# First two query units of the memory attention: multiplying the sum before its norm, with the norm settled on their outputs

## The chip, the cores and the metric

The kernel runs on one core of one Trainium2 chip. The metric is the device time of one execution, in microseconds (us). Below, TensorE is PE, its weight load PEld, VectorE DVE, ScalarE ACT, GpSimd POOL and SyncE SP.

## What is computed

Two transformer layers follow one another on a sequence of 256 tokens of width 1024. Only this part of the first layer matters here:

```python
h = hybrid_mixer(x, ...)                        # ends in  concat @ w_out
x = layer_norm(ALPHA * x + h, ln1_g, ln1_b)     # the first norm
h = memory_cross_attention(x, mem, wq, wkv, wo) # q = x @ wq, softmax(q k^T / 16) v @ wo
x = layer_norm(ALPHA * x + h, ln2_g, ln2_b)
```

with `layer_norm(x) = (x - mean) * rsqrt(var + eps) * g + b`, the mean and variance of a token taken over its 1024 values. The result is needed in f32 quality.

## The kernel before

**Tiling.** Activations lie transposed: 128 rows of the width by 256 tokens, eight such blocks (`k` = 0 to 7) for the 1024 values. `X` holds the stream in f32. Each input of a product is split into a high and a low half in the matmul's own format (`INH`, `INL`, or `HIH`, `HIL`), and each weight chunk likewise (`hir`, `lor`), so that one product is three matmuls: high by high, high by low, low by high (`three`, L521).

**Weights.** A weight chunk is 512 KB: four blocks of 128 rows by 256 columns, loaded by SP to one of six buffers `raw`, rounded by ACT to `hir` (L1103), and the rest taken by DVE to `lor` (L1608, `split`). There are four `hir`/`lor` slots. A unit, such as `("xq", 0)`, is two chunks and makes 256 output columns in one PSUM bank: 48 matmuls. The class `Ahead` sets, on ACT and on DVE alike, at which place of the program a split stands: before the work on a unit's output, up to three chunks further on (`AHEAD = 3`), as far as a slot is free in the order of the program. Between them lie 48 chunks of `mod_wT`, which DVE multiplies and sums (L1625). The order on each engine is so fixed by the text; an engine that waits for one instruction holds all behind it.

**The stretch.** Four `wout` units end the mixer. After each one DVE adds its output to `X` (`resid`, L1611), ACT squares the sum (L1250), and DVE keeps running sums over the blocks (`stats`). In `layer_norm("n1")` PE then sums the columns (`row_sums`), DVE works out mean and factor on 2 columns (L1878 to L1886), PE spreads each to a bank of 256 tokens (`spread_bank`), DVE subtracts the one and multiplies by the other (L1608, `X<-X,ps`), ACT applies gain and bias twice, once to `INH` (L1269) and once to `X` (L1274), and DVE takes the low half `INL`. Then come the query units: `xq 0` and `xq 1` interleaved block by block, so that PE has 12 matmuls for each block of `x1`, then `xq 2` and `xq 3`. DVE copies each output to `QC` (L1926). From there the four heads of the attention go through a chain from PE (logits `lx`) to DVE (maximum, L1939), ACT (exponential, L1294), DVE (L1943, scaling) and PE.

The third norm, before the second layer, already does what the change brings here, in a larger form: its units `("q", 2)` and `("k", 2)` multiply `X` by a gain (`xg`, `late_g`), and the norm is settled on the outputs (L2127 to L2131, L1405).

Of the kernel before, what the change touches and what calls it, by code (L numbers as in the profile page):

```python
# [14 lines left out]
T = 256  # L15
# [310 lines left out]
UNITS = ((0, 1), (1, 1), (2, 2), (4, 2), (6, 2))  # L326


def build(nc, A, out):
    with ExitStack() as ctx:  # L330
# [19 lines left out]
        HIH = sb("HIH", 22 * TE, F32R)[:, :].rearrange("p (k t) -> p k t", t=TE)[:, :, 0:T]  # L350
        HIL = sb("HIL", 22 * TE, F32R)[:, :].rearrange("p (k t) -> p k t", t=TE)[:, :, 0:T]
# [83 lines left out]
        SN = SMALL[:, 424:436]  # L435
        SS, VP, VR4, SD4, RR = (CH[:, a:a + n] for a, n in ((0, 4), (4, 2), (6, 2), (8, 2), (10, 2)))
# [12 lines left out]
        xg = Inp("xg", INHX, INLX)  # L449
        mem, hid, hd = (Inp(n, HIH, HIL) for n in ("mem", "hid", "hd"))  # L450
# [32 lines left out]
        def last_matmul(i):  # L483

            (key, k0), _, n, kind = plan[i]
            if k0 + n < ends[key]:
                return "read", i
            return ("unit", key, 1) if kind == "wide" or key in (("q", 2), ("k", 2)) else ("unit", key)
# [24 lines left out]
        def tensor(e):  # L513
# [24 lines left out]
            def units_g(keys, kt, x, outs=columns):  # L538
                bs = [lin.get(("unit", key), bank) for key in keys]
# [29 lines left out]
            def unit(key, kt, x, outs=columns):  # L569
                run(units_g([key], kt, x, outs))  # L570
# [30 lines left out]
            def late_g(keys, x, n):  # L601
                bs = [[p.get(("unit", key, j), bank, hold=True) for j, p in enumerate((lin, att))] for key in keys]
                w.wait_ge(act.at(("xg", "hi ext")), dve.at(("xg", "lo ext")))
# [201 lines left out]

            for c in range(4):
                unit(("wout", c), 8, mix)
            mm.mark("x1 free")
            layer_norm("n1")

            mm.mark("before cross attention")
            run(units_g([("xq", 0), ("xq", 1)], 8, x1))
            unit(("xq", 2), 8, x1)
            unit(("xq", 3), 8, x1)
            mm.mark("oc free")

            for i in range(6):
                if i < 4:
                    b, before = att.get(("lx", i), bank)
                    w.wait_ge(copied(before), dve.at(("QC", i)), act.at("KV"))  # L820
# [262 lines left out]
        def scalar(e):  # L1083
# [192 lines left out]

            for c in range(4):
                ahead.unit(("wout", c), 8)
                square("n1", c, X[:, 2 * c:2 * c + 2, :], dve.at(("n1", "x", c)), squares_free("n1", None, c))
                if c == 2:  # L1280
                    preload(ACT.Sqrt)
            layer_norm("n1", "ln1_g", "ln1_b", x1, "x1 free")

            act.mark("before cross attention")
            ahead.units([("xq", 0), ("xq", 1)], 8)
# [317 lines left out]
        def vector(e):  # L1603
# [310 lines left out]

            for c in range(4):
# [3 lines left out]
            layer_norm("n1", "ln1_g", "ln1_b", x1, "x1 free")  # L1919

            dve.mark("before cross attention")
            before = [mm.at("before cross attention"), dve.at("before cross attention"), act.at("before cross attention")]

# [680 lines left out]
```

## Time and profile before

| | us |
|---|---|
| median of three runs | 903.06 |
| lowest and highest of them | 900.4, 904.37 |
| the profiled execution | 901.49 |
| its span, first to last instruction | 899.7 |

| engine | busy, share of the span |
|---|---|
| PE | 95% |
| PEld | 90% |
| DVE | 72% |
| ACT | 56% |

Shares are averages over stages with different limits. In the chain of work that ended last, PE has 63% of the span, DVE 14% and ACT 7%. What the change is worth is read in its own stretch, some 40 us from the last `wout` unit to the first maximum of the attention.

### The profile page before, as it was taken

What the parts mean: (1) busy time and instruction counts of PE and PEld (TensorE: products, weight loads), DVE (VectorE), ACT (ScalarE), POOL (GpSimd) and SP (SyncE); (2) the same over time, 40 slices, a digit from 0 to 9 for tenths busy, and PEclk for the clock granted to TensorE, in tenths of its full rate; (3) what the DMA queues carried; (4) which work ended last, traced back from release to release, by engine and by line L of the source; (5) the groups of instructions that cost most, each with busy time, mean ns of one, the idle gap of its engine ahead of it and who ended that gap; (6) DMA issues with size and microseconds to landing.
All of it is one profiled execution on the core that took longest, in us unless ns stands there. A gap on an engine that the chain in (4) does not pass through costs nothing.

```text
span 899.7 us, 15840 instructions
## 1 busy us (share of the span) xinstructions
PE 857.0 (95%) x6396; PEld 807.8 (90%) x6396; DVE 651.3 (72%) x1011; ACT 503.2 (56%) x723; POOL 7.6 (1%) x17
## 2 busy tenths in 40 slices
PE   8989998999899999999997989999899899999997
PEld 7869987889799999999996989898899899999886
DVE  5765697678668888887867896687797866665453
ACT  5644447355447666655446657777657654444442
POOL 0200000000000000000000000000000000000000
PEclk9989999989998999999988999999999799999999
DMA  9973567747062766567752576475575276775751
GB/s 337 241 226 104 160 229 221 212 154 238 24 184 74 231 186 185 174 208 255 260 188 70 154 222 200 129 224 166 160 225 175 66 250 219 233 233 186 162 212 47
DMA packets 139592, 166.89 MB, mean 186 GB/s; under 512 B 5520, under 2 KB 123280, under 8 KB 139520
## 3 DMA queue, kind: packets, MB, share of 16 engines
q1 hardware_dynamic: 137712, 162.82, 57.8%
q0 software_dynamic: 720, 2.02, 1.2%
q8 instruction: 50, 0.82, 0.4%
q10 hardware_dynamic: 1088, 1.05, 0.3%
q14 instruction: 22, 0.18, 0.1%
HBM read 164.62 MB, written 1.25 MB: 184 GB/s over the span
## 4 chain that ended last, share of the span: by engine, by line
PE 63%; DVE 14%; ACT 7%; issue 3%; DVEq 0%; ACTq 0%
PE ps L519 62%; DVE lor L1608 5%; DVE FA L1608 3%; ACT hir L1103 2%; DVE FA L1611 1%; DVE FA L1614 1%; DVE X L1608 1%; DVE INL L1608 1%; DVE raw L1625 0%; ACT FA L1294 0%; ACT L1447 0%; ACT FA L1227 0%; ACT FA L1489 0%; DVE X L1611 0%; ACT L1118 0%
## 5 line engine op out<-in xcount | busy, mean ns | idle before, releaser
L1608 DVE TENSOR_TENSOR lor<-raw,hir 128x1024 fp32r<-128x1024 f32 (+1 forms) x267 | 309.8, 1177 | 115.2 <-ACT hir L1103 110.2
L1103 ACT ACTIVATE hir<-raw 128x1024 fp32r<-128x1024 f32 (+1 forms) x257 | 260.3, 1032 | 124.9 <-PE ps L519 104.4
L519 PE MATMUL ps<-INH,hir 128*128 128x256 f32 (+1 forms) x1064 | 306.7, 288 | 4.2 <-ACT INH L1269 2.5
L519 PE MATMUL ps<-INH,lor 128*128 128x256 f32 (+1 forms) x1064 | 302.5, 284 | 3.4 <-DVE lor L1608 3.4
L519 PE MATMUL ps<-INL,hir 128*128 128x256 f32 (+1 forms) x1064 | 303.2, 285 | 1.2 <-DVE INL L1608 0.9
L519 PEld LDWEIGHTS ps<-INH,hir 128*128 128x128 f32 x1064 | 204.7, 192 | 7.4 <-issue 5.8
L519 PEld LDWEIGHTS ps<-INH,lor 128*128 128x128 f32 x1064 | 204.4, 192 | 5.4 <-DVE lor L1608 4.4
L519 PEld LDWEIGHTS ps<-INL,hir 128*128 128x128 f32 x1064 | 204.0, 192 | 2.5 <-DVE INL L1608 2.4
L519 PE MATMUL ps<-HIH,lor 128*128 128x256 f32 x688 | 195.9, 285 | 4.3 <-DVE lor L1608 4.3
L519 PE MATMUL ps<-HIH,hir 128*128 128x256 f32 x688 | 198.2, 288 | 0.0
L519 PE MATMUL ps<-HIL,hir 128*128 128x256 f32 x688 | 194.6, 283 | 0.0
L519 PEld LDWEIGHTS ps<-HIH,lor 128*128 128x128 f32 x688 | 131.0, 190 | 6.1 <-DVE lor L1608 5.3
L519 PEld LDWEIGHTS ps<-HIH,hir 128*128 128x128 f32 x688 | 131.3, 191 | 3.9 <-issue 3.0
L519 PEld LDWEIGHTS ps<-HIL,hir 128*128 128x128 f32 x688 | 131.6, 191 | 0.0
L1611 DVE SCALAR_TENSOR_TENSOR FA<-ps,vec,FA 128x254 f32<-128x254 f32 (+2 forms) x130 | 53.2, 473 | 15.2 <-ACT FA L1113 15.2
L519 PE MATMUL ps<-hir,HIH 128*128 128x512 f32 (+1 forms) x136 | 52.8, 388 | 6.5 <-DVE HIL L1608 6.5
L1625 DVE SCALAR_TENSOR_TENSOR raw<-raw,cb 128x1024 f32<-128x1024 f32 x48 | 58.2, 1218 | 0.6 <-DMA raw<-in_mod_wT 0.6
L519 PE MATMUL ps<-lor,HIH 128*128 128x512 f32 (+1 forms) x136 | 52.3, 384 | 0.0
L519 PE MATMUL ps<-hir,HIL 128*128 128x512 f32 (+1 forms) x136 | 52.2, 384 | 0.0
L1113 ACT ACTIVATE FA<-ps,vec 128x256 f32<-128x256 f32 x58 | 29.3, 556 | 30.4 <-PE ps L519 30.4
L519 PE MATMUL ps<-FA 128*128 128x256 f32 (+6 forms) x212 | 39.2, 365 | 4.2 <-DVE FA L1608 3.4
L1608 DVE TENSOR_TENSOR HIL<-FA,HIH 128x512 fp32r<-128x512 f32 (+2 forms) x34 | 23.4, 689 | 23.8 <-ACT HIH L1108 23.2
(270 smaller groups left out, 792.8 us busy)
## 6 DMA issues: line engine op xcount, KB each, us to landing
raw<-in_w_in SPq DMA_DIRECT2D x64, 512.0 KB, 4.7
raw<-in_mod_wT SPq DMA_DIRECT2D x48, 512.0 KB, 4.5
raw<-in_ffn_w_up SPq DMA_DIRECT2D x44, 512.0 KB, 4.6
raw<-in_w_ffn_in SPq DMA_DIRECT2D x44, 512.0 KB, 4.7
raw<-in_w_ffn_out SPq DMA_DIRECT2D x22, 512.0 KB, 4.6
raw<-in_ffn_w_down SPq DMA_DIRECT2D x20, 512.0 KB, 4.8
raw<-in_xa_wkv SPq DMA_DIRECT2D x16, 512.0 KB, 4.2
raw<-in_xa_wq SPq DMA_DIRECT2D x8, 512.0 KB, 4.9
```

The costliest lines, as they stand in the source:

```text
L519: return e.matmul(o, l, r, start=start, stop=stop, skip_group_check=True)
L1103: e.activation(hi, src, ACT.Copy).then_inc(*w_hi.up(i))
L1113: e.activation(o[:, b, :], p[:, b * T:(b + 1) * T], ACT.Identity, scale=V(wname, (K - 1) * nb + i + b), bias=V(bname, i + b)).then_inc(*ac ...
L1608: return e.tensor_tensor(o, a, b, op)
L1611: return e.scalar_tensor_tensor(out=o, in0=a, scalar=s, in1=b, op0=op0, op1=op1)
L1614: return e.tensor_scalar(o, a, s1, s2, op0, op1) if op1 else e.tensor_scalar(o, a, s1, None, op0)
L1625: e.scalar_tensor_tensor(out=v, in0=v, scalar=1.0, in1=CB[:, :], op0=MUL, op1=MUL, accum_out=MOD[:, key[1]:key[1] + 1]).then_inc(*dve.up(key))
```

## The change

The first two query units no longer read the normed `x1` but a new input `xg1` = `X` times `ln1_g`, before the norm. With G = diag(g), the query is ((x - mean) / dev * g + b) W = (x G W - mean * (g W)) / dev + b W. Two extra columns beside the 256 tokens hold g and b themselves, so that the same matmuls (258 columns) give gW and bW.

- **In the `wout` loop**, after each unit ACT makes two blocks of `xg1.hi` (128x256 each, `gained`) and DVE the two of `xg1.lo`. Before the loop ACT and DVE each write the two extra columns (`gains`). `xg1` lies in `HIH`/`HIL`, blocks 0 to 7.
- **PE** runs one step of the two units (12 matmuls: two units, two halves of 128 columns) before the column sums, one between sums and mean, one between mean and factor, and five behind it. Each unit uses two banks, one of `lin`, one of `att`.
- **The norm itself stays**, since `x1` is needed by `xq 2`, `xq 3` and the residual. It goes in four pairs of blocks instead of 1, 1, 2, 2, 2; the mean row is copied by ACT to `MB` first; gain and bias of all eight blocks are applied to `X` by ACT, none by DVE.
- **The splits** of the following weight chunks stand at other places: one and a `mod` product before the first subtraction, two and a `mod` product between the second and the third pair, one behind the norm, one between the two settlings.
- **Settling**, per unit, replaces the copy to `QC` (128x512): DVE does a copy of two columns and a 128x256 multiply-subtract for each half, then a 128x512 multiply; ACT negates and adds bW, twice 128x256. The logits of heads 0 and 1 wait for ACT's part.

The core of the diff:

```diff
+        xg1, xg2 = (Inp(n, HIHX[:, 0:8, :], HILX[:, 0:8, :]) for n in ("xg1", "xg2"))
...
+            def late_norm(name, keys, x):
+
+                g = late_g(keys, x, 2)
+                steps_of(g, 1)
+                row_sums(name, 3, X[:, 6:8, :])
+                steps_of(g, 1)
+                spread_bank((name, "mu"), SN[:, 0:2])
+                steps_of(g, 1)
+                spread_bank((name, "r"), SN[:, 6:8])
+                run(g)
...
-            layer_norm("n1")
-
             mm.mark("before cross attention")
-            run(units_g([("xq", 0), ("xq", 1)], 8, x1))
+            late_norm("n1", LATE[0], xg1)
             unit(("xq", 2), 8, x1)
-            unit(("xq", 3), 8, x1)
+            unit(("xq", 3), 8, x1, pool=att)
+            late_free(LATE[0])
```

ACT, and below it DVE:

```diff
+            def gained(x, name, gn, c, free):
+                for k in (2 * c, 2 * c + 1):
+                    w.wait_ge(dve.at((name, "x", c)), vec_in.at(0), mm.at(free))
+                    e.activation(x.hi[:, k, 0:T], X[:, k, :], ACT.Copy, scale=V(gn, k)).then_inc(*act.up((x.name, "hi", k)))
...
+                for k in (0, 2, 4, 6):
+                    if k == 4:
+                        run(late)
...
+            def settle(i, key, dst):
+                for j in range(2):
+                    w.wait_ge(dve.at((key, "normed")))
+                    e.activation(dst[:, j, :], dst[:, j, :], ACT.Identity, scale=-1.0, bias=GB2[i][j][:, 1:2]).then_inc(*act.up((key, "settled")))
...
+            for c in range(2):
+                settle(c, ("xq", c), QC[:, 2 * c:2 * c + 2, :])
+                if c == 0:
+                    ahead.more()
```

```diff
+                for k in (0, 2, 4, 6):
+                    d = X[:, k:k + 2, :]
+                    w.wait_ge(act.at((name, "mean row")), act.at((x.name, "hi", k + 1)), dve.at((x.name, "lo", k + 1)))
+                    tt(d, d, over(MB, 2), SUB).then_inc(*dve.up())
+                    w.wait_ge(mm.at((name, "r")), dve.last())
+                    tt(d, d, over(br[:, 0:T], 2), MUL).then_inc(*dve.up((name, "normed", k), ("out", (name, "r"))))
+                    if k:
+                        low(k - 2)
+                    if k == 2:
+                        run(late)
+                low(6)
+                ahead.more()
...
-            query(0)
-            query(1)
```

The order on the engines follows from this. PE, from the end of the last `wout` unit; before:

```order
L519 MATMUL ps<-HIL,hir 128x256
L519 MATMUL ps<-con,st 128x1
L519 MATMUL ps<-con,SQ 128x1
L519 MATMUL ps<-con,st 128x1
L519 MATMUL ps<-con,SQ 128x1
L519 MATMUL ps<-con,X 128x1 x4
L519 MATMUL ps<-con,SQ 128x1 x4
L519 MATMUL ps<-con,small 128x128 x4
L519 MATMUL ps<-INH,hir 128x256
```

PE at the same place after the change:

```order
L523 MATMUL ps<-HIL,hir 128x258
L523 MATMUL ps<-con,st 128x1
L523 MATMUL ps<-con,SQ 128x1
L523 MATMUL ps<-con,st 128x1
L523 MATMUL ps<-con,SQ 128x1
L523 MATMUL ps<-con,X 128x1 x4
L523 MATMUL ps<-con,SQ 128x1 x4
L523 MATMUL ps<-HIH,hir 128x258
```

Twelve matmuls of 258 columns now stand ahead of the column sums, and twelve between them and the spreading of the mean; `con,small` is a spread.

ACT from the first normed block to the table load for the exponential; before:

```order
L1269 ACTIVATE INH<-X,vec 128x256 x4
L1274 ACTIVATE X<-X,vec 128x256 x2
L1269 ACTIVATE INH<-X,vec 128x256 x2
L1274 ACTIVATE X<-X,vec 128x256 x2
L1269 ACTIVATE INH<-X,vec 128x256 x2
L1274 ACTIVATE X<-X,vec 128x256 x2
L1103 ACTIVATE hir<-raw 128x1024 x7
L1294 ACT_TABLE_LOAD
```

ACT after the change, from the second pair of blocks on:

```order
L1322 ACTIVATE INH<-X,vec 128x256 x2
L1326 ACTIVATE X<-X,vec 128x256 x2
L1124 ACTIVATE hir<-raw 128x1024 x2
L1322 ACTIVATE INH<-X,vec 128x256 x2
L1326 ACTIVATE X<-X,vec 128x256 x2
L1322 ACTIVATE INH<-X,vec 128x256 x2
L1326 ACTIVATE X<-X,vec 128x256 x2
L1124 ACTIVATE hir<-raw 128x1024
L1333 ACTIVATE FA<-FA,small 128x256 x2
L1124 ACTIVATE hir<-raw 128x1024
L1333 ACTIVATE FA<-FA,small 128x256 x2
L1124 ACTIVATE hir<-raw 128x1024 x3
```

Two of the seven splits moved ahead of the third pair, and each settling (`FA<-FA,small`) stands between splits.

DVE behind the last low halves of `x1`; before:

```order
L1608 TENSOR_TENSOR INL<-X,INH 128x2x256 x2
L1625 SCALAR_TENSOR_TENSOR raw,small<-raw,cb 128x1024
L1608 TENSOR_TENSOR lor<-raw,hir 128x1024 x2
L1625 SCALAR_TENSOR_TENSOR raw,small<-raw,cb 128x1024
L1926 COPY FA<-ps 128x512 x2
L1608 TENSOR_TENSOR lor<-raw,hir 128x1024 x2
L1625 SCALAR_TENSOR_TENSOR raw,small<-raw,cb 128x1024
L1608 TENSOR_TENSOR lor<-raw,hir 128x1024
L1926 COPY FA<-ps 128x512
L1608 TENSOR_TENSOR lor<-raw,hir 128x1024 x2
L1926 COPY FA<-ps 128x512
L1939 TENSOR_REDUCE small<-ps 128x2
```

DVE after the change; behind these rows come the multiply that ends the second settling, a `mod` product, a split, the copy of `xq 2`, two splits, the copy of `xq 3` and the first maximum:

```order
L1670 TENSOR_TENSOR INL<-X,INH 128x2x256 x2
L1670 TENSOR_TENSOR lor<-raw,hir 128x1024
L2027 COPY small<-ps 128x2
L1673 SCALAR_TENSOR_TENSOR FA<-st,small,ps 128x256
L2027 COPY small<-ps 128x2
L1673 SCALAR_TENSOR_TENSOR FA<-st,small,ps 128x256
L1670 TENSOR_TENSOR FA<-FA,ps 128x512
L1670 TENSOR_TENSOR lor<-raw,hir 128x1024
L2027 COPY small<-ps 128x2
L1673 SCALAR_TENSOR_TENSOR FA<-st,small,ps 128x256
L2027 COPY small<-ps 128x2
L1673 SCALAR_TENSOR_TENSOR FA<-st,small,ps 128x256
```

The two copies of queries 0 and 1 became two settlings of five instructions each, and three splits that stood behind them now stand elsewhere: two before the third pair, one between the settlings.

## Rows read from the trace of the kernel before

**Rows 1.** The page: busy time, share of the span and instructions of each engine.

```profile
PE 857.0 (95%) x6396; PEld 807.8 (90%) x6396; DVE 651.3 (72%) x1011; ACT 503.2 (56%) x723; POOL 7.6 (1%) x17
```

**Rows 2.** Windows: start:end, length, then busy time of each engine, granted clock.

```profile
167.60:190.40 22.80, 22.80 (x194) 22.75 (x193) 17.85 (x24) 12.09 (x15) 0.00 (x0) 1.00 0.84 254
190.40:197.50 7.10, 5.15 (x34) 4.43 (x32) 3.76 (x12) 2.38 (x4) 0.00 (x0) 0.77 0.50 150
222.90:238.00 15.10, 12.42 (x63) 10.10 (x63) 8.66 (x24) 6.17 (x20) 0.00 (x0) 1.00 0.23 82
```

**Rows 3.** Timeline, PE: start us, busy us, what; column sums, spreads, first query matmul.

```profile
191.86 1.05 PE L519 MATMUL ps<-con,X 128*128 128x1 f32 x8 [0.51 <-DVE X L1611]
...
194.06 2.25 PE L519 MATMUL ps<-con,small 128*128 128x128 f32 x8 [0.26 <-DVE small L1878]
197.56 0.55 PE L519 MATMUL ps<-INH,hir 128*128 128x256 f32 x1 [1.24 <-ACT INH L1269]
```

**Rows 4.** Timeline, DVE, from the last residual to the first maximum.

```profile
188.85 2.36 DVE L1608 TENSOR_TENSOR lor<-raw,hir 128x1024 fp32r<-128x1024 f32 x2 [0.57 <-ACT hir L1103]
191.13 0.68 DVE L1611 SCALAR_TENSOR_TENSOR X<-X,ps 128x512 f32<-128x512 f32 x1
193.85 0.16 DVE L1878 COPY small<-ps 128x4 f32<-128x4 f32 x1 [2.04 <-PE ps L519]
194.87 0.17 DVE L1886 RECIPROCAL small<-small 128x2 f32<-128x2 f32 x1 [0.27 <-ACT small L1264]
...
203.77 1.40 DVE L1608 TENSOR_TENSOR X<-X,ps 128x512 f32<-128x512 f32 x2
...
207.53 0.69 DVE L1608 TENSOR_TENSOR INL<-X,INH 128x512 fp32r<-128x512 f32 x1 [1.76 <-ACT X L1274]
...
222.92 0.69 DVE L1926 COPY FA<-ps 128x512 f32<-128x512 f32 x1 [0.36 <-PE ps L519]
224.64 0.69 DVE L1939 TENSOR_REDUCE small<-ps 128x2 f32<-128x512 f32 x1 [1.04 <-PE ps L519]
```

**Rows 5.** Timeline, ACT: table load and splits of the loop's end, the norm, the splits.

```profile
186.30 1.28 ACT L1118 ACT_TABLE_LOAD   x1
187.70 1.99 ACT L1103 ACTIVATE hir<-raw 128x1024 fp32r<-128x1024 f32 x2
191.84 0.63 ACT L1250 ACTIVATE SQ<-X 128x512 f32<-128x512 f32 x1 [2.15 <-DVE X L1611]
...
201.83 1.08 ACT L1269 ACTIVATE INH<-X,vec 128x256 fp32r<-128x256 f32 x2
202.94 1.09 ACT L1274 ACTIVATE X<-X,vec 128x256 f32<-128x256 f32 x2
```

**Rows 6.** Timeline, PE at the third norm: sums, matmuls after them, spreads, a wait.

```profile
467.99 0.95 PE L519 MATMUL ps<-small,X 128*128 128x3 f32 x8
...
470.58 0.43 PE L519 MATMUL ps<-INH,hir 128*128 128x260 f32 x1
...
474.35 0.28 PE L519 MATMUL ps<-INH,hir 128*128 128x260 f32 x1
...
477.38 0.61 PE L519 MATMUL ps<-con,small 128*128 128x128 f32 x4
```

**Rows 7.** Timeline, DVE and ACT at the third norm: gained blocks, one settling.

```profile
455.36 0.87 DVE L1611 SCALAR_TENSOR_TENSOR INL<-X,small,INH 128x256 fp32r<-128x256 f32 x2
...
497.60 0.15 DVE L2127 COPY small<-ps 128x3 f32<-128x3 f32 x1
...
499.50 0.15 DVE L2127 COPY small<-ps 128x3 f32<-128x3 f32 x1
```

**Rows 8.** Timeline, ACT at the third norm: gained blocks, row copy, settling.

```profile
452.08 0.90 ACT L1362 ACTIVATE INH<-X,small 128x256 fp32r<-128x256 f32 x2
...
476.16 0.60 ACT L1374 ACTIVATE st<-ps 128x512 f32<-128x512 f32 x1 [1.99 <-PE ps L519]
...
502.51 1.71 ACT L1405 ACTIVATE FA<-FA,small 128x256 f32<-128x256 f32 x4 [6.56 <-DVE FA L1611]
```

More of the change, by code:

```diff
@@ L487, in last_matmul @@
                 return "read", i
-            return ("unit", key, 1) if kind == "wide" or key in (("q", 2), ("k", 2)) else ("unit", key)
+            return ("unit", key, 1) if kind == "wide" or any(key in keys for keys in LATE) else ("unit", key)
         before_in_slot, seen = {}, {}
@@ L536, in halves, with units_g @@
                 return act.at((x.name, "hi", k)), dve.at((x.name, "lo", k))
-            def units_g(keys, kt, x, outs=columns):
-                bs = [lin.get(("unit", key), bank) for key in keys]
+            def units_g(keys, kt, x, outs=columns, pool=lin):
+                bs = [pool.get(("unit", key), bank) for key in keys]
                 oo = [outs(b) for b, _ in bs]
@@ L567, in units_g, with unit @@
                         yield
-            def unit(key, kt, x, outs=columns):
-                run(units_g([key], kt, x, outs))
+            def unit(key, kt, x, outs=columns, pool=lin):
+                run(units_g([key], kt, x, outs, pool))
             def wide_g(key, kt, x, pool=lin, apart=0):
@@ new lines, in settle @@
+            def settle(name, i, key, dst, *free):
+                br = bank[name, "r"]
+                for j in range(2):
+                    b, vs = bank["unit", key, j], GB2[i][j]
+                    w.wait_ge(mm.at(("unit", key, j)))
+                    e.tensor_copy(vs, b[:, T:T + 2]).then_inc(*dve.up())
+                    w.wait_ge(dve.last(), act.at((name, "mean row")), *free)
+                    stt(dst[:, j, :], MB, vs[:, 0:1], b[:, 0:T], MUL, SUB).then_inc(
+                        *dve.up(("out", ("unit", key, j))))
+                w.wait_ge(dve.last(), mm.at((name, "r")))
+                tt(dst, dst, over(br[:, 0:T], 2), MUL).then_inc(*dve.up((key, "normed"), ("out", (name, "r"))))
@@ L1915, in vector @@
+            gains(xg1, "ln1_g", "ln1_b")
             for c in range(4):
@@ L1918, in vector @@
                 stats("n1", c, None)
-            layer_norm("n1", "ln1_g", "ln1_b", x1, "x1 free")
+                gained(xg1, "ln1_g", c)
             dve.mark("before cross attention")
             before = [mm.at("before cross attention"), dve.at("before cross attention"), act.at("before cross attention")]
+            late_norm("n1", xg1, x1, "x1 free", LATE[0])
+            for c in range(2):
+                settle("n1", c, ("xq", c), QC[:, 2 * c:2 * c + 2, :], *before)
+                if c == 0:
+                    ahead.more()
             def query(c):
```

71 lines of the change are left out of this document (64 added, 7 removed).

## The prediction

> **What bounds the kernel now.** I read the page first: PE is busy 95% of the span, DVE 72%, ACT 56% [rows 1]. The windows then say where this stretch differs. In the `wout` units PE is busy without a gap at full clock; in the 7.1 us of the norm it does little, and its mean granted clock is 0.77 [rows 2]. The PE timeline shows that hole from its side: column sums at 191.86, spreads at 194.06, the first query matmul at 197.56 after 1.24 us of waiting for ACT's first normed block [rows 3]. This is what the change fills. But the timelines of the other two engines have to be read on to the first maximum of the attention at 224.64 [rows 4]. Behind it, to 238, PE has 12.4 of 15.1 us busy by short pieces, and PE, DVE and ACT wait for each other in turn, with each head's maximum, exponential and scaling in one chain [rows 2]. That chain starts with DVE's maximum, which stands behind all of DVE's work of the stretch. So the time is set by when DVE reaches it, and whatever moves that start moves the end of the kernel by as much: nothing of the order behind it is changed. Before, DVE came to it early: it waited 0.36 us for the last query unit and 1.04 us for the logits [rows 4].
>
> **Durations used.** In a row of independent instructions each takes its busy time less some 0.09 us. A split is 1.14 us on DVE (two at 2.36) and 0.95 on ACT (two at 1.99) [rows 4, 5]. A 128x512 operation of DVE is 0.61, and 0.70 where the next depends on it (1.40 for two) [rows 4]. A gained block is 0.40 on ACT and 0.40 on DVE [rows 7, 8]. Gain and bias of a pair of blocks are four ACT instructions of 0.50, some 2.1 us [rows 5]. One settling on DVE is 1.9 us, from 497.60 to 499.50; ACT's half of it takes 0.85, half of the 1.71 for two units [rows 7, 8]. Here the settling is one instruction shorter in its second part, not in these 1.9.
>
> **Part 1, the `wout` loop.** ACT gets 8 gained blocks, DVE 8: 3.2 us on each, and 0.3 for the extra columns. In the first loops idle time hides most: DVE waits there for ACT and PE. What counts is the last loop. The 2 gained blocks of unit 2 stand ahead of ACT's table load (1.28 us) and that ahead of two splits; and the gained blocks of the two loops before have by then made the third residual 0.9 us late, since DVE's waits there don't hide all of them. ACT's splits start at 189.3 instead of 187.70 [rows 5]. DVE's two splits follow, 190.4 to 192.7, and the last residual starts at 192.7 instead of 191.13 [rows 4]: **+1.5**. PE meanwhile does its first 12 matmuls and the early column sums, so its wait costs nothing. Column sums end at 195.3, and DVE's copy comes at 195.35 against 193.85; its two last gained blocks lie in that wait.
>
> **Part 2, mean and factor.** PE now runs 12 matmuls ahead of each spread. After the column sums of the third norm the granted clock fell to the lower of its two levels, 1.2 of 2.4 GHz: from 470.58 to 474.35 17 matmuls took 3.8 us, 0.22 each; then 0.12 each [rows 6]. I take the same here, since sums and waits last from 192.4 to 195.3. The mean is spread after 12 slow matmuls, at 197.9, and ACT's copy of the row (bounded by 0.60 for twice the size, I take 0.46) ends at 199.2 [rows 8]. The factor comes after 12 more, partly slow, at 200.4, with its spread (0.61 [rows 6]) done at 201.0. DVE in the meantime has done one split and one `mod` product, to 198.7. It subtracts at 199.2 and multiplies at 201.0. Before, the third pair's subtraction and multiplication, the last ones, began at 203.77 and six blocks were done [rows 4]; now at 201.6 only two are. With the clock at full the factor would come 1.6 earlier.
>
> **Part 3, the rest of the norm.** ACT has 2.1 us for each pair, all eight blocks, and it is in series with DVE: pairs one and two take it from 201.7 to 206.0. Only then do the two splits of `xq 2` stand in its queue, 206.0 to 207.9. DVE, done with the first low half at 204.6, waits **2.5 us** for the first of them. Then two splits and the `mod` product run from 207.1 to 210.5, ahead of the last two pairs; the last low half starts at 216.3 against 207.53 before [rows 4]. Of that, 3.4 us are splits that stood behind the norm before; 5.4 are the late start and the waits.
>
> **Part 4, settling.** DVE: split of `xq 3` at 217.3 (ACT's half from 216.2), settling 0 from 218.4 to 220.3. ACT's part of it runs to 221.3; the next split is behind it in ACT's queue, and DVE waits for that until 222.4: **2.1 us**. Split to 223.5, settling 1 to 225.4, `mod` product to 226.6; ACT's part of settling 1 again stands ahead of its split, so DVE waits 0.9. Split 227.5 to 228.6, copy of `xq 2` 0.6, two splits 2.3: the copy of `xq 3` starts at 231.5 and the maximum at 232.1.
>
> **PE in the same stretch.** Its late units end at 208.1; `xq 2` begins at 208.4 and waits for low halves at 212.6, 214.9 and 217.1; `xq 3` waits for its second chunk until 223.6 and ends at 226.7, or 228.3 if the clock falls in the waits. With some 1.9 us of logits PE is done before DVE's maximum at 232.1: PE's own delay costs nothing. The SP queue is no bound: a chunk is loaded when the split six chunks ahead of it is done, and the first `xo` chunk, due at 227.5, is asked for at 208.3.
>
> **The sum.** 232.1 - 224.64 = **+7.5 us**. As a balance: +1.5 late residual; DVE work added behind it 0.8 (two gained blocks) + 3.8 (settlings) - 1.2 (two copies) - 1.1 (smaller pieces of the norm, two affine steps) = +2.3; waits of DVE 11.2 us against 7.5 before (5.5 of them in [rows 4]), +3.7. Against the profiled execution 901.49 + 7.5 = 909.0; against the median of 903.06 it is 910.5, and I take 910.0 between them. Bounds: with no clock loss after the sums 5.9, with twice as long a one 8.1. If row and split times err by 0.1 us in each of the dozen handovers, another 1.2 either way.
>
> **Rivals.**
> - **The hole fills and PE sets the time (faster).** PE's work from 190.41 is 192 matmuls of 0.12 (23.0), sums 2.9, spreads 1.1 and 1.6 for the slow clock: end at 219.0 instead of 222.9, **-3.9**, 898.5. It holds if DVE and ACT keep ahead of PE. For it: PE is the busiest engine and the hole is real [rows 1, 3]. Against it: DVE has 28.3 us of work from the late residual at 192.7 on (the 33.5 us of before less 7.5 of waits, plus 2.3), so even without any wait it reaches the maximum only at 221.0. Chance 0.08. The Trainium skill says the same as this rival (Perfetto Trace Analysis, Identifying the Most-Contended Engine and Optimization Strategy): optimize the engine with the highest occupancy first, and for TensorE by its weight-load share; find its gaps and make what it waits for start sooner. By that rule the change gains; the rows of DVE speak against it, since the engine that is late next is not the one with the gap.
> - **Waits of ACT and DVE overlap better (between).** If the two waits behind ACT's gain work and settling (2.5 and 2.1) are half as long and the clock holds, +3 to +5, 904.5 to 907.5 on the median's scale. It decides if ACT's queue is emptier than I count: its pairs at 2.1 us are measured [rows 5]. Chance 0.16.
> - **The change does nothing that can be seen.** The late units would have to hide exactly what they add. Chance 0.04.
> - **More is lost.** PE's waits of 2 to 3 us at `xq 2` and `xq 3` lower the clock; with late reads ACT's splits for `xo` come later, and low clock into the attention adds to its short matmuls: +10 to +12, 913 to 915. The clock stood at 1.00 there before [rows 2]. Chance 0.06.
>
> **How the numbers follow.** My forecast, +6 to +9, has the remaining 0.66. What a measurement of this kernel can tell from no change is about 0.5%, 4.5 us. Slower by more: 0.66 + 0.06 + a part (0.06) of the between case = 0.78. Within: 0.10 of that case, 0.04 and 0.01 of the first = 0.15. Faster: 0.07. The range of 8 in 10 leaves out the gain and the far end: 905 to 914.
>
> **What would show it.** In the changed profile: the last residual of the loop 1.5 us later relative to the end of `wout`; PE busy through most of the old hole, with matmuls of 258 columns at 0.42 us busy after the sums; DVE idle for `hir` 2 to 3 us ahead of the splits between the second and third pair, and again 2 us between the settlings; the last copy of a query unit on DVE with no wait for PE ahead of it, and the first maximum some 41.5 us after the last `wout` matmul instead of 34. Wrong, if PE's last query matmul is what the maximum waits for, or if ACT's splits stand ready when DVE comes to them.

## The result and the profile after

| | us |
|---|---|
| before, median of eight runs | 902.76 |
| after, median of eight runs | 911.06 |
| ratio, 95% interval | 1.009, 1.0067 to 1.0114 |
| profiled execution of after, and its span | 909.77, 908.0 |

The change makes the kernel slower by 0.9%, some 8.1 us. A second measurement, beside other runs of before, gave 911.21 and the ratio 1.0107 (1.0087 to 1.0127), 9.6 us.

The page of after, busy time and share of each engine, beside [rows 1]: every share is within 1 point of before, and the time is 8 us longer. The shares alone tell nothing here.

```profile
PE 859.7 (95%) x6396; PEld 810.5 (89%) x6396; DVE 655.7 (72%) x1024; ACT 509.1 (56%) x740; POOL 7.6 (1%) x17
```

More is told by the windows of the stretch, from DVE's last residual to its first maximum. The columns are those of [rows 2]. First before, then after:

```profile
191.13:224.64 33.51, 31.34 (x227) 29.78 (x228) 25.52 (x42) 17.81 (x25) 0.00 (x0) 0.90 0.58 188
```

```profile
191.90:232.91 41.01, 34.71 (x229) 32.68 (x227) 27.87 (x47) 21.23 (x34) 0.00 (x0) 0.88 0.45 143
```

DVE has 2.35 us more work in it and waits 13.1 us instead of 8.0. PE's busy time grew by 3.4 us for nearly the same number of matmuls (229 against 227), with a mean granted clock of 0.88 instead of 0.90.

The timeline of DVE in after, from the last residual to the first maximum (start, busy time, what; in brackets the wait ahead and who ended it). It answers [rows 4]:

```profile
191.90 0.68 DVE L1673 SCALAR_TENSOR_TENSOR X<-X,ps 128x512 f32<-128x512 f32 x1
195.56 0.16 DVE L1992 COPY small<-ps 128x4 f32<-128x4 f32 x1 [1.00 <-PE ps L523]
199.62 0.69 DVE L1670 TENSOR_TENSOR X<-X,st 128x512 f32<-128x512 f32 x1 [0.58 <-ACT st L1315]
201.61 0.69 DVE L1670 TENSOR_TENSOR X<-X,ps 128x512 f32<-128x512 f32 x1 [1.30 <-PE ps L523]
...
207.75 2.36 DVE L1670 TENSOR_TENSOR lor<-raw,hir 128x1024 fp32r<-128x1024 f32 x2 [2.47 <-PE ps L523]
...
216.98 0.69 DVE L1670 TENSOR_TENSOR INL<-X,INH 128x512 fp32r<-128x512 f32 x1 [1.42 <-ACT X L1326]
...
223.16 1.23 DVE L1670 TENSOR_TENSOR lor<-raw,hir 128x1024 fp32r<-128x1024 f32 x1 [2.02 <-ACT hir L1124]
...
228.30 1.23 DVE L1670 TENSOR_TENSOR lor<-raw,hir 128x1024 fp32r<-128x1024 f32 x1 [0.88 <-ACT hir L1124]
229.44 0.69 DVE L2050 COPY FA<-ps 128x512 f32<-128x512 f32 x1
230.05 2.35 DVE L1670 TENSOR_TENSOR lor<-raw,hir 128x1024 fp32r<-128x1024 f32 x2
232.31 0.69 DVE L2050 COPY FA<-ps 128x512 f32<-128x512 f32 x1
232.91 0.68 DVE L2060 TENSOR_REDUCE small<-ps 128x2 f32<-128x512 f32 x1
```

The last two copies of query units and the maximum have no wait ahead of them: PE had been done. The 2.47 us are put down to PE, though the splits' `hir` halves were ACT's work from 206.57 on, behind the gain and bias of the second pair (in the trace of run 4 the same wait of 2.47 us is put down to ACT). ACT in after, the places where it stands in DVE's way:

```profile
206.57 1.99 ACT L1124 ACTIVATE hir<-raw 128x1024 fp32r<-128x1024 f32 x2
...
221.18 0.91 ACT L1333 ACTIVATE FA<-FA,small 128x256 f32<-128x256 f32 x2 [3.28 <-DVE FA L1670]
221.99 1.04 ACT L1124 ACTIVATE hir<-raw 128x1024 fp32r<-128x1024 f32 x1
```

PE in after, beside [rows 3]: a wait for the last split, sums of columns, the second late step, spreads, and at last the attention's first transposes (L853) and the matmuls behind them.

```profile
190.95 0.36 PE L523 MATMUL ps<-HIH,hir 128*128 128x258 f32 x1 [0.63 <-ACT hir L1124]
...
192.63 1.19 PE L523 MATMUL ps<-con,X 128*128 128x1 f32 x8
193.68 1.84 PE L523 MATMUL ps<-con,SQ 128*128 128x1 f32 x8
195.39 0.56 PE L523 MATMUL ps<-HIH,hir 128*128 128x258 f32 x1
...
198.11 1.05 PE L523 MATMUL ps<-con,small 128*128 128x128 f32 x4
...
200.97 0.61 PE L523 MATMUL ps<-con,small 128*128 128x128 f32 x4
...
235.76 1.12 PE L853 MATMUL ps<-con,FA 128*128 128x128 f32 x4 [4.88 <-DVE FA L1676]
236.67 3.62 PE L523 MATMUL ps<-FA 128*128 128x256 f32 x8
```

The hole is filled, and PE's gap now lies in front of the attention: it waits 4.88 us, and then its short pieces take twice the time (the eight matmuls of one head 3.62 us, against 1.89 at full clock).

**One frame for all runs.** The last `wout` matmul starts anywhere from 189.1 to 193.2 us in the profiled executions (part of why, see the last section). So all positions below count from the start of the last `wout` matmul, 190.28 before and 189.33 after. From there the first maximum stands at 34.4 before and 43.6 after, **+9.2**; the third maximum at 39.8 and 51.0, **+11.2**. The expectations below count from another matmul, at 190.04, the sixth of the late units: their positions ("42.9") are to be read 0.7 us larger; their differences and times stand.

### The profile page after: what moved, and what is told of

It is laid out like the page before. It is cut to its first block, busy times and chain, and to the rows that moved or that the text cites. A ratio compares the mean times of both kernels' runs of the same rounds, so it can differ in the third digit from the quotient of the medians.

```text
span 908.0 us, 15870 instructions
## 1 busy us (share of the span) xinstructions
PE 859.7 (95%) x6396; PEld 810.5 (89%) x6396; DVE 655.7 (72%) x1024; ACT 509.1 (56%) x740; POOL 7.6 (1%) x17
## 3 DMA queue, kind: packets, MB, share of 16 engines
q0 software_dynamic: 720, 2.02, 1.1%
q10 hardware_dynamic: 1088, 1.05, 0.3%
## 4 chain that ended last, share of the span: by engine, by line
PE 57%; DVE 17%; ACT 9%; issue 4%; DVEq 0%; ACTq 0%
PE ps L523 56%; DVE lor L1670 6%; DVE FA L1670 3%; ACT hir L1124 3%; DVE FA L1673 2%; DVE FA L1676 1%; DVE raw L1687 1%; DVE INL L1670 1%; ACT L1509 1%; DVE X L1670 1%; DVE X L1673 0%; ACT FA L1248 0%; ACT FA L1356 0%; ACT FA L1551 0%; PE ps L765 0%
## 5 line engine op out<-in xcount | busy, mean ns | idle before, releaser
L523 PE MATMUL ps<-INH,hir 128*128 128x256 f32 (+1 forms) x1032 | 297.5, 288 | 4.1 <-ACT hir L1124 1.4
L523 PE MATMUL ps<-INL,hir 128*128 128x256 f32 (+1 forms) x1032 | 294.6, 285 | 4.0 <-DVE INL L1670 3.9
L523 PE MATMUL ps<-INH,lor 128*128 128x256 f32 (+1 forms) x1032 | 294.0, 285 | 3.5 <-DVE lor L1670 3.2
L523 PE MATMUL ps<-HIH,lor 128*128 128x256 f32 (+1 forms) x720 | 205.0, 285 | 4.2 <-DVE lor L1670 4.2
L523 PE MATMUL ps<-HIH,hir 128*128 128x256 f32 (+1 forms) x720 | 208.0, 289 | 0.6 <-ACT hir L1124 0.6
L523 PEld LDWEIGHTS ps<-INH,hir 128*128 128x128 f32 x1032 | 198.7, 193 | 7.1 <-issue 4.6
L523 PE MATMUL ps<-HIL,hir 128*128 128x256 f32 (+1 forms) x720 | 203.7, 283 | 0.0
L523 PEld LDWEIGHTS ps<-INH,lor 128*128 128x128 f32 x1032 | 198.1, 192 | 6.1 <-DVE lor L1670 5.1
L523 PEld LDWEIGHTS ps<-HIH,lor 128*128 128x128 f32 x720 | 137.3, 191 | 6.0 <-DVE lor L1670 5.3
L523 PEld LDWEIGHTS ps<-HIH,hir 128*128 128x128 f32 x720 | 137.6, 191 | 4.7 <-issue 3.0
```

Of the source, the lines that this page charges most:

```text
L523: return e.matmul(o, l, r, start=start, stop=stop, skip_group_check=True)
```

## Experiments

Each row: last residual, first and third maximum and a later mark, in us behind the last `wout` matmul (from the one profiled execution of each kernel), then the median, and the ratio to before with its interval. Runs 1 to 4, 5 to 8 and 9 to 12 each were measured on one chip and share their runs of before (medians 901.29, 900.62 and 901.42). The mark is the start of DVE's first reduction over 128x8 elements, well behind the attention; in before:

```profile
345.32 0.16 DVE L1972 TENSOR_REDUCE small<-small 128x1 f32<-128x8 f32 x1
```

| kernel | residual | first max. | third max. | mark | median | ratio (95%) |
|---|---|---|---|---|---|---|
| before | 0.8 | 34.4 | 39.8 | 155.0 | | |
| after | 2.6 | 43.6 | 51.0 | 166.8 | 911.06 | 1.0090 (1.0067 to 1.0114) |
| 1 splits behind the norm | 2.6 | 41.0 | 46.4 | 163.2 | 909.80 | 1.0087 (1.0058 to 1.0117) |
| 2 split ahead of settlings | 2.6 | 41.4 | 48.9 | 165.4 | 910.23 | 1.0097 (1.0065 to 1.0129) |
| 3 table load first | 3.0 | 44.0 | 51.5 | 167.2 | 910.79 | 1.0099 (1.0072 to 1.0125) |
| 4 no steps between sums and spreads | 2.6 | 42.0 | 48.9 | 165.4 | 910.84 | 1.0105 (1.0084 to 1.0127) |
| 5 no settling | 2.5 | 36.4 | 41.8 | 157.1 | 904.47 | 1.0033 (1.0011 to 1.0054) |
| 6 before, gained blocks added | 2.6 | 38.2 | 43.6 | 159.0 | 903.14 | 1.0020 (1.0005 to 1.0035) |
| 7 before, DVE work added | 0.8 | 36.7 | 44.1 | 159.5 | 904.29 | 1.0044 (1.0031 to 1.0057) |
| 8 four moves | 1.9 | 36.4 | 41.8 | 158.3 | 903.20 | 1.0030 (1.0015 to 1.0045) |
| 9 PE busy ahead of attention | 2.6 | 43.6 | 49.0 | 165.5 | 912.11 | 1.0123 (1.0101 to 1.0146) |
| 10 after again | 2.6 | 43.6 | 51.0 | 167.0 | 911.21 | 1.0107 (1.0087 to 1.0127) |
| 11 before, `mod` products moved | 0.8 | 34.3 | 39.8 | 155.2 | 901.41 | 1.0002 (0.9986 to 1.0019) |
| 12 seven moves | 1.9 | 32.6 | 38.1 | 153.9 | 899.91 | 0.9984 (0.9966 to 1.0001) |

**The theory** is that of the prediction: the time follows the moment at which DVE has worked off its queue up to the first maximum. Rival A: PE sets it. Rival B: the loss is PE's low clock.

### 1 to 4: one wait or term at a time

**1. Splits behind the norm.** On ACT, and alike on DVE:

```diff
                 for k in (0, 2, 4, 6):
-                    if k == 4:
-                        run(late)
...
+                run(late)
                 ahead.more()
```

> The changed kernel with the two splits and the `mod` product between the second and the third pair of the norm moved behind the fourth, on ACT and on DVE. Theory (the first maximum comes when DVE has worked off its queue, and two waits of DVE for ACT, 2.5 and 2.1 us, are part of the loss): the wait of 2.47 us for the first split of `xq 2` goes, the first maximum comes about 2.5 us earlier than the 42.9 us it now lies behind the last `wout` matmul (40.4), time about 908.6. Rival A (PE sets the time once the hole is filled): PE gets the splits of `xq 2` later, so nothing is gained or 1 to 2 us lost, 911 to 913. Rival B (what is lost is the low clock of PE, in the norm and in the attention): no change, 911.

Measured: the first maximum at 41.0, 2.6 earlier than after; the third even 4.6 earlier, because PE's clock was full in the attention here. The wait of 2.47 us is gone; the one of 2.02 stands. Median 909.80 against 901.29 of before.

**2. Second split of `xq 3` ahead of both settlings.** On both engines:

```diff
+            ahead.more()
             for c in range(2):
                 settle(...)
-                if c == 0:
-                    ahead.more()
```

> The changed kernel with the second split of `xq 3` ahead of both settlings instead of between them, on ACT and on DVE. Theory: the wait of 2.02 us behind ACT's part of settling 0 goes, the first maximum 2.0 us earlier (40.9 us behind the last `wout` matmul), time about 909.0. Rival A (PE sets it): PE is through with `xq 3` sooner by the same 2 us and its logits too, so the time falls as well, but then the maximum waits for PE. Rival B (clock): PE idles longer ahead of the attention or as long, no gain in the attention, 910 to 911.

Measured: first maximum 2.2 earlier (2.0 expected), the third 2.1. The 2.02 us are gone from DVE's timeline.

**3. Table load ahead of the loop.**

```diff
             gains(xg1, "ln1_g", "ln1_b", "xg1 free")
+            preload(ACT.Sqrt)
             for c in range(4):
...
-                if c == 2:
-                    preload(ACT.Sqrt)
```

> The changed kernel with ACT's table load for the square root ahead of the `wout` loop instead of in its third turn, behind the gained blocks of unit 2. Theory (term 1 of the sum: gained blocks and table load stand ahead of two splits, and so make the last residual late by 1.5 us): last residual 1.2 to 1.5 us earlier relative to the last `wout` matmul, the first maximum as much, time about 909.7. Rival: the residual has another cause (DVE's own gained blocks), or the norm is bound by PE's sums and steps, and the gain ends there: 911. If the splits at the loop's start become late for PE by the load, the end of `wout` itself moves out by up to 1.3 us and eats it.

Measured: the residual did not come earlier, it came 0.45 later, and the maximum with it. At the loop's head ACT's splits wait for the load as well (first split at 170.51 behind the load of 169.11): the first three residuals come 1.1 us later than in after, and the last still 0.45, though the load is gone from the third turn. Where it costs nothing is found in run 12.

**4. No late steps between sums and spreads.**

```diff
                 row_sums(name, 3, X[:, 6:8, :])
-                steps_of(g, 1)
                 spread_bank((name, "mu"), SN[:, 0:2])
-                steps_of(g, 1)
                 spread_bank((name, "r"), SN[:, 6:8])
```

> The changed kernel with the late units' steps between column sums and mean and between mean and factor moved behind both spreads (one step ahead of the sums, seven behind). Theory (term 2: the 24 matmuls, slow ones at 0.22, hold mean and factor back): mean row 2.2 us and factor 3.3 us earlier, but DVE then has its split and `mod` product of 2.4 us ahead of the first subtraction, so the first maximum comes 1.6 us earlier, time about 909.4. PE's hole is partly open again, at no cost. Rival A (PE sets it): the matmuls pushed behind cost up to 2.5 us, 911 to 913. Rival B (clock): PE idle between the spreads, the low clock lasts longer, no gain.

Measured: first maximum 1.6 earlier, as expected; that PE's hole is partly open again costs nothing there, which speaks against rival A.

What the four show: three of the four positions moved as the theory has them, to 0.2 us. The times don't resolve it: with four executions each their intervals are 4 to 6 us wide, and against after's +8.1 (or +9.6, run 10) each of them allows no gain, and nearly as well the expected one. Taken together they show none: the medians of runs 1, 2 and 4 lie 8.5, 8.9 and 9.5 us above before, the two of after 8.3 and 9.8, where 2.0 us less was expected on average. Rival B and "the end doesn't follow the maximum" are so not ruled out by these times. The traces speak for the theory as far as the mark: there the three stand 3.6, 1.4 and 1.4 us earlier than after, of 4.6, 2.1 and 2.1 at the third maximum. Behind the mark the executions differ for other reasons (last section). So the next runs are larger doses.

### 5 to 8: larger doses

**5. No settling.** ACT's part is left out, and on DVE:

```diff
-                    e.tensor_copy(vs, b[:, T:T + 2]).then_inc(*dve.up())
-                    w.wait_ge(dve.last(), act.at((name, "mean row")), *free)
-                    stt(dst[:, j, :], MB, vs[:, 0:1], b[:, 0:T], MUL, SUB).then_inc(
+                    w.wait_ge(act.at((name, "mean row")), *free)
+                    e.tensor_copy(dst[:, j, :], b[:, 0:T]).then_inc(
...
-                tt(dst, dst, over(br[:, 0:T], 2), MUL).then_inc(*dve.up((key, "normed"), ("out", (name, "r"))))
```

> The changed kernel without the settling: the outputs of `xq 0` and `xq 1` are copied to the queries as they are (two copies of 128x256 each), and ACT's part is left out. This leaves out mean, deviation and bias of heads 0 and 1. Theory (term 4: two settlings on DVE, 3.8 us less two copies, and the waits of 2.0 and 0.9 us behind ACT's parts): the first maximum 5.5 us earlier than in the changed kernel, 37.4 us behind the last `wout` matmul, 3 us later than before; time about 3 us above before. Rival A (PE sets the time): no change from the changed kernel, 8 us above before. Rival B (the end of the kernel doesn't follow the first maximum, as the four runs so far, all between 7.9 and 9.5 us above before, could also be read): 8 us above before with the maximum early.

Measured: first maximum at 36.4, 7.2 us earlier than after (5.5 expected), time +3.0 us (1.0 to 4.9) against before. Both rivals had 8. This is the largest single part of the loss, and the time follows the maximum. (The profiled execution was one of the fastest, 899.38 in a range of 899.27 to 908.22, with twelve in all.) DVE from residual to maximum:

```profile
191.74:225.62 33.88, 30.92 (x225) 29.91 (x223) 25.35 (x41) 19.54 (x30) 0.00 (x0) 0.90 0.53 163
```

Of the 7.2 us, 2.5 are work (27.9 to 25.4) and 2.9 the two waits behind ACT's parts. Most of the other 1.8 isn't the settling's: the copy of the sums came 2.72 us behind the residual instead of 3.66, as with column sums at full clock, and the 0.58 us of waiting for the mean row went too.

**6. The gained blocks alone, in the kernel before.** ACT, and alike DVE with its multiply-subtract:

```diff
                 square("n1", c, X[:, 2 * c:2 * c + 2, :], dve.at(("n1", "x", c)), squares_free("n1", None, c))
+                gained(xg1, "n1", "ln1_g", c, "xg1 free")
```

> The kernel before with the sixteen gained blocks of the `wout` loop alone (eight on ACT, eight on DVE), which nothing reads. Term 1 of the sum says: last residual 1.5 us later relative to the last `wout` matmul. After it the order is the old one, where the norm follows the residual directly and PE waits for it: the mean comes 1.5 us later plus what the two last gained blocks of DVE (0.87) and ACT (0.9) add on the way to the sums. First maximum 1.5 to 2.5 us later than before, time 1.5 to 2.5 us longer. Rival: the loop's waits hide it all, 0.

Measured: residual 1.7 later, time +1.8 us (0.5 to 3.1). In this execution the maximum is 3.8 us later, more than the 1.5 to 2.5 that I expected: the copy of the sums comes 4.34 us behind the residual instead of 2.72. Position and time don't agree here: 3.8 lies outside the interval of the time. From 192.3 to 205.9 us the granted clock was at its lower level here (mean 0.50; 0.75 before in the same stretch); how it stood in the other eleven executions isn't shown.

**7. Seven more copies on DVE, in the kernel before.** 

```diff
             def query(c):
...
+                for _ in range(7 if c == 2 else 0):
+                    e.tensor_copy(QC[:, 2 * c:2 * c + 2, :], wide2(bank["unit", ("xq", c)])).then_inc(*dve.up())
+                    then("again")
```

> The kernel before with the copy of query unit 2 made eight times instead of once, each waiting for the one ahead: some 4.9 us more on DVE ahead of the first maximum, and nothing on the other engines. It tests the ground of the whole sum. Theory (the end of the kernel follows DVE's first maximum one to one): 4.9 less the waits of 0.36 and 1.04 us that it fills, so the maximum 3.5 to 3.9 us later, and the end as much; if PE's longer idle stretch ahead of the attention lowers its clock there, up to 2 us more. Rival: slack behind the attention takes it up, 0 to 1.5 us.

Measured: the copies took 5.03 us. The maximum is only 2.4 later (3.5 to 3.9 expected), since the padding also filled a third wait (1.06 us for ACT's `hir`, at 221.33). But the third maximum is 4.3 later, and the time +4.0 us (2.8 to 5.1). PE in this kernel:

```profile
229.85 1.12 PE L832 MATMUL ps<-con,FA 128*128 128x128 f32 x4 [3.54 <-DVE FA L1614]
230.76 3.62 PE L519 MATMUL ps<-FA 128*128 128x256 f32 x8
```

So what DVE's work adds beyond the waits that it fills is paid at the end, and PE, made to wait 3.54 us, then ran its first pieces at half the clock: 2.0 us on top. This run needs nothing of the change to lose 4 us.

**8. Four moves at once**: runs 1, 2 and 4, and the table load behind the gained blocks of the fourth turn instead of the third.

> The changed kernel with four moves at once: splits of `xq 2` behind the norm, second split of `xq 3` ahead of the settlings, ACT's table load in the fourth turn of the `wout` loop behind the gained blocks (instead of in the third), no late steps of PE between column sums and spreads. Theory (DVE's queue sets; waits of 2.5, 2.0, the 1.5 of the residual and part of the 1.6 of the spreads go): first maximum about 5.2 us earlier than in the changed kernel, time 3 to 4 us above before. It can't beat before, since DVE has 2.3 us more to do there. Rival (the end doesn't follow the maximum): 8 us above before.

Measured: maximum 7.2 us earlier than after (5.2 expected), time +2.7 us (1.4 to 4.1), from +8. DVE's window from residual to maximum:

```profile
192.48:227.01 34.53, 32.09 (x229) 30.55 (x227) 27.69 (x48) 22.46 (x36) 0.00 (x0) 0.90 0.53 169
```

Its work is nearly that of after (27.7 against 27.9), its waits are down to 6.8 from 13.1. The gains of runs 1, 2 and 4 (2.6, 2.2 and 1.6) add up, with 0.7 for the load (7.1 in all). What is left is the added work and part of the late residual.

### 9 to 12: the clock, and a version without the loss

**9. PE kept busy ahead of the attention.**

```diff
+                    w.wait_ge(copied(before))
+                    for _ in range(18 if h == 0 else 0):
+                        mul(b[:, 0:128], C("ident"), C("ones"))
-                    w.wait_ge(copied(before), dve.at(("PX", h)))
+                    w.wait_ge(dve.at(("PX", h)))
```

> The changed kernel with eighteen matmuls on constants (128x128, f32) ahead of PE's first transposes of the attention, into the bank that these then overwrite, so that PE is busy in most of the 4.88 us in which it waits for DVE's first scaling. Theory on the clock (the granted clock falls in that idle time, the next three short blocks of PE work take about twice as long, and the third maximum comes 2.0 us late for it): the third maximum stands 5.4 us behind the first, as in the kernel before, instead of 7.4; the time is 2 us shorter than the changed kernel's, 6 us above before. Rival: the extra matmuls are in the way or the clock is low anyway, no gain or up to 1 us lost.

PE in this kernel, ahead of and in the attention:

```profile
232.03 4.18 PE L523 MATMUL ps<-con 128*128 128x128 f32 x36
237.07 0.66 PE L856 MATMUL ps<-con,FA 128*128 128x128 f32 x4 [0.86 <-DVE FA L1679]
237.56 1.89 PE L523 MATMUL ps<-FA 128*128 128x256 f32 x8
```

Measured: the pieces run at full clock and the third maximum stands 5.4 us behind the first instead of 7.4, exactly the 2.0. Its cause, PE's idle time ahead of the pieces, is so shown. But the time shows no gain: 912.11 against 911.21 of after on the same chip (run 10), five runs each. The traces lose it on the way: the 2.0 us are 1.8 at DVE's copy of the second norm's sums (87.2 against 88.9 us behind the last `wout` matmul), 1.5 at the mark and 1.2 at the kernel's end (719.6 against 720.8). Against the first execution of after, whose end is at 718.6, the lead is gone. How much of it a median holds is open.

**10. After, unaltered.**

> The changed kernel once more, unaltered, as the mark beside which the others of this call are read: 8.3 us above before (ratio 1.009), first maximum 42.9 us behind the last `wout` matmul.

Measured: ratio 1.0107, 9.6 us, first maximum at 43.6 as in the first execution, the mark at 167.0 (166.8). From the mark to the end this execution took 553.8 us and the first one 551.8, with the same kernel: the 14 executions have 550.9 to 554.4 there.

**11. The `mod` products moved, in the kernel before.**

```diff
-    add2(("xq", 0), A["xa_wq"], 0, ("xq", 1), A["xa_wq"], 256, mod=1)
+    add2(("xq", 0), A["xa_wq"], 0, ("xq", 1), A["xa_wq"], 256)
     for c in (2, 3):
-        add(("xq", c), A["xa_wq"], 256 * c, 8, mod=1)
+        add(("xq", c), A["xa_wq"], 256 * c, 8)
     for c in range(4):
-        add(("xo", c), A["xa_wo"], 256 * c, 8)
+        add(("xo", c), A["xa_wo"], 256 * c, 8, mod=int(c < 3))
```

> The kernel before with the three `mod` products of the query units (3.4 us of DVE) at the `xo` units instead, where DVE waits 2.4 us in each unit; nothing else is changed. Theory: before, PE's last query matmul is what the first maximum waits for (0.36 and 1.04 us), so DVE's relief buys nothing: maximum the same within 0.5 us, time 0 to 1 us shorter. Rival: DVE's work is what counts before too, 3 us shorter.

Measured: maximum at 34.3 (34.4), time the same, +0.2 us (-1.3 to 1.7). Before, DVE had enough slack: relief alone gives nothing.

**12. Seven moves**: the changed kernel with the moves of run 8, those of run 11, and two on ACT:

```diff
+                if c == 3:
+                    preload(ACT.Sqrt)
                 square("n1", c, X[:, 2 * c:2 * c + 2, :], dve.at(("n1", "x", c)), squares_free("n1", None, c))
                 gained(xg1, "n1", "ln1_g", c, "xg1 free")
...
             settle(0, ("xq", 0), QC[:, 0:2, :])
             ahead.unit(("xq", 2), 8)
             settle(1, ("xq", 1), QC[:, 2:4, :])
```

> The four moves of the kernel with the +2.7 us (splits behind the norm, second split of `xq 3` ahead of the settlings, no late steps between sums and spreads, ACT's table load out of the way) and three more: the table load stands ahead of the fourth square, where ACT waits 3 us anyway; ACT makes the first `xo` split between its two settling parts, so that DVE doesn't wait 0.88 us for it; the three `mod` products of the query units stand at the `xo` units. DVE then has 5.1 us less ahead of the maximum. Theory (DVE's queue was the bound, and with it off PE's filled hole becomes the gain that the change was worth): PE runs from the spreads to the last query matmul nearly without a gap and is now what the maximum waits for; the maximum 4.5 to 5 us earlier than with the four moves, 3 to 4 us earlier than before relative to the `wout` units; time 2 to 3.5 us below before (ratio 0.996 to 0.998). Rival (something behind the attention, such as the `mod` products now at the `xo` units or the splits there, takes it back): level with before or 1 us above.

Measured: first maximum at 32.6, 1.7 us earlier than before and 3.8 earlier than with four moves (4.5 to 5 expected); time 899.91 against 901.42, ratio 0.9984 (0.9966 to 1.0001), 1.4 us less with an interval that just reaches no change. DVE from residual to maximum, then PE's only waits from the spreads to the logits:

```profile
195.11:225.85 30.74, 29.20 (x222) 28.36 (x221) 25.60 (x43) 21.22 (x34) 0.00 (x0) 0.94 0.49 152
```

```profile
211.25 0.39 PE L523 MATMUL ps<-INH,hir 128*128 128x256 f32 x1 [0.32 <-ACT hir L1122]
212.60 0.39 PE L523 MATMUL ps<-INH,lor 128*128 128x256 f32 x1 [0.97 <-DVE lor L1666]
```

DVE's work is back at that of before (25.6 against 25.5), and now DVE and PE come to the maximum together. DVE's last copy ends at 225.85; PE's first logits begin at 223.93, and the maximum follows 1.92 us behind, as before (222.72 and 224.64). DVE, then PE:

```profile
225.16 0.69 DVE L2044 COPY FA<-ps 128x512 f32<-128x512 f32 x1
225.85 0.69 DVE L2054 TENSOR_REDUCE small<-ps 128x2 f32<-128x512 f32 x1
```

```profile
223.93 3.62 PE L523 MATMUL ps<-FA 128*128 128x256 f32 x16
```

One `mod` product still landed ahead of the maximum (at 222.88), but the missing 1 us isn't its doing: without it the maximum would still wait for the logits. PE itself gained little. From the end of the last `wout` unit to the logits it idles 1.5 us against 2.2 before; the other 1.1 of its 1.7 us is less busy time for the same 227 matmuls, at a mean granted clock of 0.94 instead of 0.89, and how long the clock is low here differs between executions anyway. With run 11 beside it, the gain is not that of moved `mod` products alone. The other moves were not all tried in the kernel before: there too the table load stands ahead of two splits and the last residual, and its new place alone might give part of the 1.4 us. So the gain is small, not certain, and not shown to be the filled hole's.

## Why the prediction was right

The forecast was 910.0 in 905 to 914, and slower by over 0.5% at 0.78; 911.06 was measured. Point by point:

- **The base** (the end follows DVE's first maximum one to one). Run 7 shows it in the kernel before, runs 5, 8 and 12 in the changed one: shifts of the first maximum of +2.1, +2.0 and -1.7 us against before (runs 5, 8, 12) went with times of +3.0, +2.7 and -1.4, and +2.4 with +4.0 in run 7. "One to one" was incomplete: a delay that makes PE wait adds the attention's low clock, which in after and run 7 is 2.0 us at the third maximum. Behind the attention nothing takes a shift up as far as the mark: every kernel stands there within 1.6 us of its shift at the third maximum, and 0 to 1.6 us later, not earlier. But the times follow it only roughly: run 6 had +3.8 with +1.8, and runs 1, 2, 4 and 9, with third maxima 2 to 4.6 us earlier than after's, gained nothing that can be seen.
- **Part 1**, +1.5: 1.7 measured, in after as in run 6. Of it 0.7 go with the table load (run 8: 1.9 instead of 2.6). The third residual was forecast 0.9 late and is (4.43 instead of 5.36 us ahead of the last `wout` matmul). But the step "in the first loops idle time hides most" doesn't hold for the first turn: the first two residuals lie 6.63 us apart instead of 5.82, so that turn hides hardly anything and the next nearly all.
- **Part 2** was mis-sized. From the last residual to the copy of the sums I had 2.65 us, 3.66 were measured. I took the column sums at full clock, 1.05 and 1.03; they took 1.19 and 1.84, at a clock that was low while they ran and not only behind them. (In other executions of the same order the copy came 2.7 to 3.9 us behind the residual, so the size is partly chance.) The 12 slow matmuls ahead of the mean (0.42 busy, one each 0.215) were as forecast, though the row that this came from has 18 matmuls between 470.58 and 474.35, not 17, the last two faster. The first multiplication came 9.7 us behind the residual instead of 8.3: 1.4 us of the 1.7 by which the sum was short.
- **Part 3**: DVE's wait 2.47 against 2.5, named at the right place, and run 1 took it away. The splits behind it and the last low half came within 0.1 us of the forecast, once part 2's 1.4 are taken off.
- **Part 4**: settling on DVE 1.9 us, then waits of 2.02 (2.1 forecast) and 0.88 (0.9). Run 2 took the first away. The whole settling is worth 5.4 us of the 7.2 of run 5 (5.5 expected for it).
- **PE's own delay is free**: right, there is no wait for PE ahead of the last copies and the maximum, and run 4 pushed PE's work behind the spreads at no loss in the maximum.
- **The balance**: late residual +1.7 (1.5), work +2.35 (2.3), waits +5.15 (3.7): +9.2 instead of +7.5.
- **The rivals.** "The hole fills and PE sets the time" fell, and with it, for this stretch, the order that the Trainium skill gives (Perfetto Trace Analysis, Identifying the Most-Contended Engine) as the prediction reads it: the busiest engine's gap was closed and the time grew. Only in run 12, where DVE was first brought back to its old load, does PE come to the maximum as late as DVE. "More is lost" named a mechanism that did occur, the low clock in the attention, which I had given 0.06: +11.2 at the third maximum.
- **Luck.** The sum was 1.7 us short at the first maximum and put the attention's clock at nothing, another 2.0; at the mark after stands 11.8 us behind before (12.0 in run 10). That the times came out at +8.1 and +9.6, close to the forecast of +7.5, is partly luck: the traces of after make up 2.6 and 0.6 us of it behind the mark, where nothing was changed, and single executions of one kernel differ by as much.

## What to carry to other kernels

Before work is moved to fill the gap of the busiest engine, add up what the engine that feeds it has from the same moment to the next place where both meet; if that sum is longer, the filled gap turns up again a little later, larger. In queues whose order the program fixes, the small additions (0.9 us of gained blocks, 0.9 us of settling) cost what stands behind them, so the place of a split is worth as much as its duration: four moves of order took 5 of 8 us back. And when times don't resolve an effect, positions in the trace can, if they are all counted from one mark just ahead of the stretch and a change of the clock is looked for between: they tell where an effect stands, not that a median will hold it.

## What the runs showed that I had not expected

**A wait of PE just ahead of short pieces.** PE waited for DVE's first scaling in every kernel, and the clock behind it (0.66 us for the four transposes at the full level of 2.4 GHz, 1.1 at the lower of 1.2) was: full after 0.86 us (run 9), 1.17 (before, runs 6, 11 and 12), 1.60 (run 5), 2.82 (run 8) and 3.06 (run 1); low after 3.35 (runs 4 and 10), 3.54 (run 7), 4.86 (run 3), 4.88 (after) and 5.04 (run 2). Where it was low, the third maximum lay 6.9 to 7.4 us behind the first, else 5.4.

**The same wait with either outcome.** In the mixer PE waits 2.67 us for DVE in every execution, until 154.17 in before, 151.64 in after and 154.26 in run 12. The windows of 6 us in or right behind it (first before, then after, then run 12; granted clock third from the end):

```profile
152.00:158.00 6.00, 3.83 (x23) 3.42 (x24) 4.79 (x14) 2.52 (x4) 0.00 (x0) 1.00 0.71 233
```

```profile
152.00:158.00 6.00, 6.00 (x25) 4.66 (x24) 3.01 (x5) 2.70 (x4) 0.00 (x0) 0.72 0.56 194
```

```profile
152.00:158.00 6.00, 3.74 (x15) 3.58 (x16) 4.36 (x13) 2.11 (x4) 0.00 (x0) 0.63 0.78 227
```

In seven of the fourteen kernels' executions (after, runs 1, 2, 3, 8, 10 and 12) the clock fell there, in the others (before, runs 4 to 7, 9 and 11) it did not, though the work up to there is the same in all. Where it fell, PE came to the `wout` units 1.5 to 1.6 us later beside before than it had been ahead of the wait, in run 12 2.7 us; where it didn't, no time was lost. It is one source of the 4 to 8 us by which single runs of one kernel differ, and the reason why no single position in these traces should be compared without a mark close by.

**A table load is free only in a wait of ACT.** 1.28 us in each case; it made the last residual later in the third turn (0.7 us) and at the head of the loop (0.45 more than that), and not at all ahead of the fourth square, where ACT still waited 1.48 us behind it for the residual.
